# Key logits of the decode group: queries in padded stationary columns, keys as the moving operand

## The reference, cut to what matters

```
qg  = q.reshape(bsz, nq, ATT_KV_HEADS, ATT_GROUP, ATT_HEAD_DIM)          # 2 kv heads x 4 query heads x 128
att = einsum('bqgrd,bqkgd->bqgrk', qg, k_sel) * ATT_HEAD_DIM ** -0.5     # for the selected keys
att = where(valid, att, -inf);  p = softmax(att);  o = einsum('bqgrk,bqkgd->bqgrd', p, v_sel)
```

## Time and profile before

| | us |
|---|---|
| median of 3 executions | 2725.63 |
| lowest and highest of them | 2719.56, 2736.84 |
| the profiled execution, its own time | 2721.79 |
| span of the profile in it | 2720.0 |

### The profile page before, as it was taken

How to read it: one execution, slowest core, us unless ns; L and a number is a source line. 1 busy time by engine, 2 the same in 40 slices (tenths; PEclk the granted TensorE clock), 3 DMA queues, 4 the chain that set the end, 5 groups by cost and what they waited for, 6 DMA issues and landing times. The chain is left out here.

```text
span 2720.0 us, 43371 instructions
## 1 busy us (share of the span) xinstructions
PE 2625.8 (97%) x16469; PEld 2519.5 (93%) x16469; DVE 1106.0 (41%) x2395; ACT 564.8 (21%) x1010; POOL 1200.9 (44%) x1524
## 2 busy tenths in 40 slices
PE   7999998999999999999889998999999999999998
PEld 7899878999999999999749996888999999999998
DVE  6959666342121121124379876554332121121223
ACT  3010244121010010111054534443120010010112
POOL 5535223655455554557303301001655455554552
PEclk9999989999999999999889987999999999999999
DMA  6535535111111111111303225202111111111111
GB/s 207 103 82 96 169 95 171 47 47 47 47 47 47 46 46 46 46 46 46 109 13 106 86 68 177 60 1 86 47 47 47 47 47 47 46 46 46 46 46 71
DMA packets 291412, 188.45 MB, mean 69 GB/s; under 512 B 41030, under 2 KB 281290, under 8 KB 290522
## 3 DMA queue, kind: packets, MB, share of 16 engines
q1 hardware_dynamic: 265590, 178.54, 21.7%
q10 hardware_dynamic: 25700, 8.32, 2.5%
HBM read 151.84 MB, written 34.98 MB: 69 GB/s over the span
## 5 line engine op out<-in xcount | busy, mean ns | idle before, releaser
L521 POOL TENSOR_TENSOR w_hi<-w_raw,ones 128x256 fp32r<-128x256 f32 x720 | 620.4, 894 | 1280.9 <-PE ps L532 1153.1
L524 POOL TENSOR_TENSOR w_lo<-w_raw,w_hi 128x256 fp32r<-128x256 f32 x720 | 536.9, 778 | 25.6
L532 PE MATMUL ps<-out_x_hi,w_hi 128*128 128x344 f32 x1920 | 409.7, 322 | 6.9 <-DVE out_x_lo L2123 6.9
L532 PE MATMUL ps<-next_hi,w_hi 128*128 128x344 f32 x1920 | 416.0, 325 | 0.0
L532 PE MATMUL ps<-next_lo,w_hi 128*128 128x344 f32 x1920 | 410.7, 322 | 0.0
L532 PE MATMUL ps<-out_x_lo,w_hi 128*128 128x344 f32 x1920 | 409.0, 321 | 0.0
L532 PE MATMUL ps<-next_hi,w_lo 128*128 128x344 f32 x1920 | 408.4, 321 | 0.0
L532 PE MATMUL ps<-out_x_hi,w_lo 128*128 128x344 f32 x1920 | 406.7, 320 | 0.0
L2148 DVE TENSOR_TENSOR resid<-ps,resid 128x344 f32 (+1 forms) x240 | 108.9, 509 | 707.5 <-PE ps L532 707.5
L532 PEld LDWEIGHTS ps<-out_x_hi,w_hi 128*128 128x128 f32 x1920 | 324.9, 189 | 7.2 <-issue 7.2
L532 PEld LDWEIGHTS ps<-next_lo,w_hi 128*128 128x128 f32 x1920 | 328.1, 191 | 0.0
(11 more groups left out here) (553 smaller groups left out, 2751.7 us busy)
## 6 DMA issues: line engine op xcount, KB each, us to landing
w_raw<-in_w_up SPq DMA_DIRECT2D x64, 512.0 KB, 4.0
w_raw<-in_w_down SPq DMA_DIRECT2D x64, 512.0 KB, 4.0
w_raw<-in_w_in SPq DMA_DIRECT2D x36, 512.0 KB, 4.6
resid_spill<-resid SPq DMA_DIRECT2D x2, 4128.0 KB, 13.7
ml_inputs<-in_ring SPq DMA_DIRECT2D x16, 516.0 KB, 3.0
resid<-resid_spill SPq DMA_DIRECT2D x4, 2064.0 KB, 7.4
w_raw<-in_w_out SPq DMA_DIRECT2D x16, 512.0 KB, 4.3
keys<-in_cache_k SPq DMA_DIRECT2D x64, 128.0 KB, 2.0
```

The lines of the kernel that those rows point to most:

```text
L521: m.nc.gpsimd.tensor_tensor(parts(hi[:, k]), x[:, k], one, ALU.mult)
L524: last = m.nc.gpsimd.tensor_tensor(parts(lo[:, k]), x[:, k], hi[:, k], ALU.subtract)
L532: ins = nc.tensor.matmul(out[c], parts(w), parts(x[:, token_cols(c)]), start=first and n == 0, stop=last and n == 2)
```

## The change

For each task the queries become the stationary operand and the keys the moving one. The queries lie in a zeroed tile `q_wide` of 1088 columns, so placed that the 64 columns of task t are zero but for its 4 queries, which stand at the columns that belong to its sequence and heads. A task has two matmuls of 512 moving columns, one for keys 0 to 511 into partitions 0 to 63 of one bank and one for keys 512 to 1023 into partitions 64 to 127. All 16 tasks add into this one bank: only the first starts it. Behind the last task ACT copies the bank to SBUF (over the queries, which are no longer needed), PE turns it by 4 transposes behind the second token block of `rows`, and DVE adds the mask in two halves. POOL clears `q_wide` at the beginning of the phase, and DVE's first write of queries waits for that.

```diff
+    ROWS = B * AH
+    q_wide = r.take(B, 2 * ROWS + AH)
+    task_queries = q_wide.rearrange("p b x -> p (b x)")
+    new_queries = lambda g: q_wide[:, :, g * (ROWS + AG):g * (ROWS + AG) + AG]
+    logit_rows = task_queries[:, 0:4 * PAGE]
...
-    s_bank, counts, news = m.ps[5], m.ps[6], m.ps[7]
+    logit_bank, turned_logits, counts, news = m.ps[5], m.ps[4], m.ps[6], m.ps[7]
...
         def _(pool):
+            nc.gpsimd.memset(q_wide, 0.0).then_inc(m.wide_clear.sem, 1)
             for u in range(2, units):
                 split_unit(pool, m, u % 2, u // 2)
...
             def key_logits(t):
                 b, g = tasks[t]
                 pe.wait_ge(m.act_b.sem, m.act_b.at(t + 1))
-                for j in range(PAGES):
-                    at = (j * B + b) * AH + g * AG
-                    last = nc.tensor.matmul(s_bank[:, at:at + AG], keys_t[t % 2][:, j], s.q_s[:, b, g * AG:(g + 1) * AG],
-                                            start=True, stop=True)
+                for half in range(2):
+                    last = nc.tensor.matmul(logit_bank[half * ROWS:(half + 1) * ROWS], task_queries[:, t * ROWS:(t + 1) * ROWS],
+                                            keys_t[t % 2][:, 4 * half:4 * half + 4].rearrange("p j k -> p (j k)"),
+                                            start=(t == 0), stop=(t == 2 * B - 1))
                 last.then_inc(m.pe_c.sem, 1)
+
+            def turn_logits():
+                pe.wait_ge(m.logits_out.sem, m.logits_out.at(1))
+                for j in range(4):
+                    last = nc.tensor.transpose(turned_logits[:, j * P:(j + 1) * P], logit_rows[:, j * PAGE:(j + 1) * PAGE],
+                                               m.ident[:])
+                last.then_inc(m.logits_turned.sem, 1)
...
             for t in range(n_blocks):
                 rows(t)
+                if t == 1:
+                    turn_logits()
...
             for t in range(BITS - first_turn, 2 * B):
                 copy_keys(t)
+            act.wait_ge(m.pe_c.sem, m.pe_c.at(2 * B))
+            act.wait_ge(m.dve_d.sem, m.dve_d.at(1))
+            nc.scalar.copy(logit_rows, logit_bank).then_inc(m.logits_out.sem, 1)
...
-                    V.tensor_tensor(s.q_s[:, :, u], banks[2][:, CH - B:CH], m.inv_rms[:, T:N], ALU.mult)
+                    if u == 0:
+                        dve.wait_ge(m.wide_clear.sem, m.wide_clear.at(1))
+                    V.tensor_tensor(new_queries(u // AG)[:, :, u % AG], banks[2][:, CH - B:CH], m.inv_rms[:, T:N], ALU.mult)
...
-            dve.wait_ge(m.pe_c.sem, m.pe_c.at(2 * B))
+            dve.wait_ge(m.logits_turned.sem, m.logits_turned.at(1))
             V.drain()
-            V.tensor_tensor(s.s_logit, s_bank[:].rearrange("p (j b h) -> p j b h", j=PAGES, b=B),
-                            s.mask_t.rearrange("p b j -> p j b").unsqueeze(3).to_broadcast([P, PAGES, B, AH]), ALU.add)
+            for half in range(2):
+                js = slice(4 * half, 4 * half + 4)
+                V.tensor_tensor(s.s_logit[:, js], turned_logits.rearrange("p (j x b h) -> p x j b h", x=2, b=B, h=AH)[:, half],
+                                s.mask_t.rearrange("p b j -> p j b")[:, js].unsqueeze(3).to_broadcast([P, 4, B, AH]), ALU.add)
```

More of the change, by code:

```diff
@@ L244, in __init__ @@
         self.states_out = signal("states_out")
+        self.wide_clear = signal("wide_clear")
+        self.logits_out = signal("logits_out")
+        self.logits_turned = signal("logits_turned")
         self.skipped = signal("skipped")
@@ L3119, in _ @@
                     for g in range(KVH):
-                        ins = V.tensor_tensor(s.new_logit[:, :, g * AG:(g + 1) * AG], s.q_s[:, :, g * AG:(g + 1) * AG],
+                        ins = V.tensor_tensor(s.new_logit[:, :, g * AG:(g + 1) * AG], new_queries(g),
                                               m.proj[:, KT1 + g, T:N].unsqueeze(2).to_broadcast([P, B, AG]), ALU.mult)
@@ L3161, in phase_topk @@
         q.passed(2 * B)
-    for q in (m.dve_d, m.dve_e, m.pe_e):
+    for q in (m.dve_d, m.dve_e, m.pe_e, m.wide_clear, m.logits_out, m.logits_turned):
         q.passed(1)
```

## The result

The changed kernel takes 2702.4 us (median of 4 executions, 2699.2 to 2702.97) where the kernel before, timed beside it, takes 2731.2 (4 executions, 2719.6 to 2737.1): ratio 0.991, 95% interval 0.9883 to 0.9937 (the quotient of the two medians alone is 0.989). Timed again later, 9 executions against 14, it is 2705.4 against 2728.4, ratio 0.9927 (0.9902 to 0.9952). The forecast was 2711 with a range of 2700 to 2728. The time lies inside, near its lower end, and the gain is larger than forecast: 28.8 us by the first pair of medians, 23.0 by the later pair and 19.9 between the two profiled spans (2720.0 and 2700.1), where 14.55 had been summed.

A forecast was written before the change was run, and what follows sets the result against it. PE alone was taken to set the pace of the ten steps, partly at 1.2 GHz. Terms 1.1 + 8.5 + 0.75 + 3.7 + 1.0 - 0.5 = 14.55 us gave a median of 2711, range 2700 to 2728.

The forecast's parts named there:

- The dips: Falls of PE's clock in the ten steps that carry tasks: all five gone, 1.7 us each, 8.5 us gained.
- The pass itself: Key logits: four passes of 512 columns at 0.42 us, 1.7 us a task; gain 1.1 us for tasks 0 to 10.
- rival of a single sweep: Key logits: a 512-column pass takes 0.216 us, each of eleven tasks 0.85 us less; time 2700; chance 0.05.
- The page wait: PE's wait for task 14's key pages: moves as a whole with task 11, SP's 8.31 us stay.
- The tail: PE turning tasks 14 and 15 and multiplying 13 to 15: 9.8 us for 13.46, gain 3.7.
- The k and v blocks and their stores: Behind the tail's multiplications: four blocks at full clock give 1.0 us, PE's added turns cost 0.5.
- The cover that ran out: Phase end: DVE's chain, 40.4 us plus 0.2, stays covered by SP's end at 42.9, with 2.3 us to spare.
- passes about 0.42 us apart: Sign of being right: a task's four key-logit passes stand about 0.42 us apart.
- a phase that ends with DVE's add: Sign of being wrong: DVE's add, not SP's last store, ends the phase.
- What was added: New work: POOL's clear 1.0 us and ACT's bank copy 0.54, both covered; PE's four turns cost 0.5.
- the dips that stay: Rival in the ten steps: turned blocks, not key logits, lower the clock; 2725, or 2718 if half stay; chance 0.20.
- the clock that falls more often: Rival: each step from 1541 on has a dip, five more, 8.5 us; time 2735; chance 0.08.

The follow-up runs named there:

- the run with shorter ranks: Changed kernel with one DVE operation less for each of six ranked prompt blocks; stretch behind the steps 40.2 us for 41.2, whole span 2709.3.

## Why the prediction was right or wrong

*The dips: right, with a wrong reason beside it.* 8.5 us were summed; the run with 64 moving columns prices them at 7.8, or 1.55 a dip for the 1.7 of the sum. The step asked whether transposes alone pull the clock down and answered no, which the trace after shows (1.00 with the same 8 transposes). That four-column passes do it as such was too wide: eight of them do not, and sixteen do not in the next phase, which the trace before could have told. The reading that PE does little else than such passes from 1634 to 1652 was loose, too: they are about 10 of the 18 us, and transposes are nearly all of the rest.

*The pass itself: wrong.* The sum had four passes of 0.42 one after the other, 1.7 us a task; measured are 1.01, and ten tasks make 7.4 us of it where the same tasks had 1.0 in the sum. This is the term that was mis-sized. The single pass was priced rightly from the earlier trace rows: it still takes 0.43 where both halves share their columns. What was missed is that the two matmuls, which write partitions 0 to 63 and 64 to 127, run at once: the sum put them one after the other, and no row that it rests on has two such matmuls. That their stationaries lie in different halves of the array is the likely reason. The Trainium skill, "TensorEngine Tiling (Array Packing)", section "Theoretical Speedup", gives a factor of up to two for a dimension of at most 64; the runs agree, 1.86 us against 1.01. My rival of a single sweep came out near in time (2700) by a mechanism that is not there, and the figure of 216 ns that stood by it is not what a pass takes here. So the time fell inside the range with some luck: the range reached down to 2700 for that rival and for the spread of the runs, not for two matmuls at once.

*The page wait: right* that it stays; 10.05 us from SP's first issue to task 14, 10.02 before. It lost its price all the same, since DVE took over the end.

*The tail: right in its way, mis-sized.* From task 14 to the new token's logits it took 7.95 us for the 9.8 of the sum and the 13.46 before. The clock came up 5.8 us behind the start of task 14, where 5.4 were assumed, and so turning 15 still took 1.9 us; but each task was cheaper. The k and v blocks and their stores gained 1.6 us, where 1.0 less 0.5 was summed.

*The cover that ran out: wrong.* DVE's chain was put at 40.4 us and 0.2 more, done 2.3 ahead of SP. Its length was right (1597.51 to 1637.96, 40.45). But SP was through 39.55 us behind the same start (1637.06), not 42.9, since its chain became 8.4 us shorter where the sum had 5.05 (the tail gave 5.5 for 3.7, the blocks and stores 1.6 for 0.5). So DVE became the end, and of SP's 8.4 us the phase got 7.7. Of the prediction's own signs, one of being right did not come (passes about 0.42 us apart), and one of being wrong did (a phase that ends with DVE's add).

*What was added* cost what was said. POOL's clear took 1.0 us, ACT's copy of the bank 0.59 (0.54 summed), and PE's four turns 0.47 from their start to the next block's (0.5):

```profile
1427.39 1.01 POOL L2892 MEMSET resid<- 128x1088 f32 x1 [0.29 <-POOLq L2624]
1444.35 2.83 POOL L524 TENSOR_TENSOR w_hi<-w_raw,ones 128x256 fp32r<-128x256 f32 x4 [15.96 <-PE ps L535]
```

```profile
1626.88 0.59 ACT L3022 COPY resid<-ps 128x512 f32<-128x512 f32 x1 [1.18 <-PE ps L2927]
1627.67 1.20 ACT L3027 COPY keys<-ps 128x256 f32<-128x256 f32 x4 [0.21 <-PE ps L2948]
```

POOL still waits 15.96 us behind its clear, and ACT waits 0.21 us for the first block behind its copy: both lie in covers, as forecast. Of the other rivals, the dips that stay and the clock that falls more often did not come.

## What to carry to other kernels

Price a matmul by the columns of its stationary and by the partitions that it writes, too: two fp32 matmuls that write 64 partitions each, 0 to 63 and 64 to 127, took 1.01 us here where they took 1.86 in the same 64. Small moving operands can cost twice, once for their own passes and once as a slower clock for whatever dense work comes behind them. They did in one phase of this kernel and not in the next, so look at the granted clock right behind such a stretch. Where two chains end a phase within a microsecond of each other, a cut in one gives at most that microsecond until the other is cut as well.

## What the runs showed of the hardware that was not expected

Which traces started the phase late was decided far ahead of it, in the index phase, whose work no edit here touches. Its clock in one and the same stretch, first of the kernel before, then of the run with shorter ranks:

```profile
1340.00:1400.00 60.00, 47.98 (x201) 27.80 (x203) 35.85 (x62) 20.45 (x48) 9.08 (x21) 0.77 0.09 21
```

```profile
1340.00:1400.00 60.00, 51.32 (x162) 28.53 (x163) 26.66 (x55) 16.52 (x38) 9.03 (x21) 0.57 0.09 19
```

The second did fewer matmuls in the same time (162 records for 201) and reached task 0's count matmul at 1553.7, where the kernel before had been there at 1541.8. One execution can so lose 10 us or more before the change is even reached, which is up to half of what the change gives; the times of the ten steps and of the stretch behind them agree within 0.1 us between those of the ten traces whose edits leave them alone. What decides how long that phase stays at 1.2 GHz was not tried.
